# Retrieval gathers in a hybrid decoder step: from 128 tokens by one pick to 64 tokens by two picks

## The reference, cut to what matters

```
pre    = einsum('thkd,td->thk', u_tab[expert], t)      # a dot product per token and pick
act    = gelu(pre) * softmax(top_s)                    # the gate of the pick
y[t]   = einsum('thk,thkd->td', act, v_tab[expert])    # weighted sum of 128 V rows
x      = x + y
```

## Time and profile before

| what | value |
|---|---|
| runs, median (lowest, highest) | 3408.7 us (3402.18, 3413.93) |
| profiled execution, span from first to last instruction | 3400.1 us |
| around the span, against the median | 8.6 us |
| PE busy | 2863.5 us (84%) |
| DVE busy | 2339.7 us (69%) |
| ACT busy | 1195.4 us (35%) |
| POOL busy | 1270.1 us (37%) |
| mean granted TensorE clock | 0.935 |
| moved by DMA | 1225.95 MB, mean 361 GB/s |

### The profile page before, as it was taken

How to read it: one execution, slowest core, us unless ns; L and a number is a source line. 1 busy time by engine, 2 the same in 40 slices (tenths; PEclk the granted TensorE clock), 3 DMA queues, 4 the chain that set the end, 5 groups by cost and what they waited for, 6 DMA issues and landing times.

```text
span 3400.1 us, 31764 instructions
## 1 busy us (share of the span) xinstructions
PE 2863.5 (84%) x9786; PEld 1646.9 (48%) x9786; DVE 2339.7 (69%) x5016; ACT 1195.4 (35%) x3524; POOL 1270.1 (37%) x1102
## 2 busy tenths in 40 slices
PE   8888997888988798787988898788789787888887
PEld 7767764555564356354732365355455232322222
DVE  4454799786778788787566787767668776755444
ACT  3211355332323432443233432432333343334333
POOL 0100233554434443444334433344334343434342
PEclk9899998997899999899999999897889899899999
DMA  4205698999999999999999999999999999999997
GB/s 158 73 8 204 246 390 313 370 375 386 393 406 420 378 413 384 374 381 399 413 421 421 387 407 387 360 345 417 365 410 411 386 419 421 383 422 419 421 422 314
DMA packets 186076, 1225.95 MB, mean 361 GB/s; under 512 B 21281, under 2 KB 23857, under 8 KB 50738
## 3 DMA queue, kind: packets, MB, share of 16 engines
q0 software_dynamic: 152976, 1114.74, 80.8%
q1 hardware_dynamic: 32930, 109.19, 8.5%
HBM read 1212.00 MB, written 11.84 MB: 360 GB/s over the span
## 4 chain that ended last, share of the span: by engine, by line
PE 42%; DMA 29%; DVE 17%; ACT 5%; issue 3%; DVEq 3%; POOL 1%; SPq 0%; ACTq 0%; POOLq 0%
PE ps L601 41%; DMA ring<-in_uv,picked 27%; DVE ring L2329 5%; DVE otok L2263 1%; DVEq L2104 1%; ACT diag L1175 1%; POOL ring L584 1%; ACT scratch L1175 1%; ACT L1175 1%; DVE scratch L2062 1%; ACT gated L1175 1%; DVE keep L1599 1%; ACT act_v L1175 1%; DMA wring<-in_weights 1%; DVE scratch L2066 0%
## 5 line engine op out<-in xcount | busy, mean ns | idle before, releaser
L601 PE MATMUL ps<-ring,diag 128*128 128x512 f32 (+1 forms) x3348 | 1715.6, 645 | 362.6 <-ACT diag L1175 350.4
L584 POOL DMA_INDIRECT ring<-in_uv,picked x1024 | 1184.9, 1157 | 1769.1 <-PE ps L601 1254.1
L2329 DVE SCALAR_TENSOR_TENSOR ring<-ring,htok 128x1024 f32<-128x1024 f32 x1024 | 1249.7, 1227 | 626.5 <-DMA ring<-in_uv,picked 619.2
L601 PEld LDWEIGHTS ps<-ring,diag 128*128 128x128 f32 (+1 forms) x3348 | 619.8, 199 | 1212.8 <-ACT diag L1175 665.7
L1175 ACT ACTIVATE act_v<-pre 128x1 f32<-128x1 f32 x1040 | 210.2, 202 | 1685.7 <-DVE ring L2329 1671.8
L601 PE MATMUL ps<-hT,wring 128*128 128x256 f32 (+1 forms) x3200 | 752.4, 390 | 26.5 <-DVE hT L1562 8.8
L601 PEld LDWEIGHTS ps<-hT,wring 128*128 128x128 f32 x3200 | 618.1, 194 | 200.6 <-issue 96.3
L1175 ACT ACTIVATE diag<-masks,gated 128x128 f32<-128x128 f32 x821 | 329.6, 402 | 27.2 <-PE ps L601 0.2
L1175 ACT ACTIVATE gated<-act_v,gates 128x1 f32<-128x1 f32 x1024 | 301.7, 295 | 33.3
L2263 DVE SCALAR_TENSOR_TENSOR otok<-ring,gated,otok 128x1024 f32<-128x1024 f32 x197 | 252.2, 1280 | 1.1 <-ACT gated L1175 1.1
L601 PEld LDWEIGHTS ps<-scratch 128*128 128x128 f32 (+2 forms) x1428 | 190.5, 196 | 99.5 <-issue 59.5
(11 more groups left out here) (337 smaller groups left out, 1521.1 us busy)
## 6 DMA issues: line engine op xcount, KB each, us to landing
wring<-in_weights SPq DMA_DIRECT2D x200, 512.0 KB
ring<-in_uv,picked POOLq DMA_INDIRECT x1024
scratch<-in_keys POOLq DMA_DIRECT2D x4, 1024.0 KB
scratch<-in_s_gla POOLq DMA_DIRECT2D x4, 1024.0 KB, 12.9
out_o_gla<-scratch POOLq DMA_DIRECT2D x4, 1024.0 KB, 11.1
scratch<-in_s_dn POOLq DMA_DIRECT2D x1, 2048.0 KB, 12.4
scratch<-in_s_ssm POOLq DMA_DIRECT2D x1, 2048.0 KB, 16.7
out_o_dn<-scratch POOLq DMA_DIRECT2D x1, 2048.0 KB, 11.1
```

The source lines that it names most:

```text
L584: pool.indirect_dma_start(out=ring[:, g % RING, :], out_offset=None, in_=io["uv"][L], in_offset=bass.IndirectOffsetOnAxis(ap=index, axis=0 ...
L601: return pe.matmul(out, lhsT, rhs, start=start, stop=stop)
L2329: stt(x, x, 1.0, h, MUL, MUL, accum_out=pre[:, g % SMALL:g % SMALL + 1]).then_inc(sem("dotted"), 1)
```

## The change

Every gather now holds 64 tokens twice: partitions 0 to 63 get one pick of the 64 tokens, partitions 64 to 127 another pick of the same 64 tokens. A unit becomes two half tiles (SUBS, 16 in all, bank w%2 for half tile w) of 64 gathers each, and the number of gathers stays 1040. In the table of picks a group of two heads gives 16 gathers. The matrix of gated values is `diag` of 128x64, made from `folded` (two 64x64 identities stacked), so one product sums both picks. The two 512-column products go to the PSUM partitions 0 to 63 (columns 0 to 511 of the V row) and 64 to 127 (columns 512 to 1023) of one bank. SHARE, add_v and join_out are gone.

What goes with it: `htok[:, 1 + w % 2]` holds the 64 rows twice, made by two 64-column products for each half row from `htok[:, 0]` (fold_rows) and two ACT copies; POOL waits for v_done alone; at the third gather of a half tile ACT copies the sums of the one before to `otok` (copy_out), at the fifth PE transposes them (turn, 4 transposes) and DVE adds them to `xT` (add_out); picks and gates are written to `ids` and copied in four pieces each (fold_choice); the sample tokens' V rows are summed by eight products with one moving column each (sample_v) and the sample rows are spread by eight 128-column products; the last half tile alone is normed in token order, 512 columns wide over all partitions; some slots move by 1 to 4 gathers.

```diff
-SHARE = {0: "21111111", 1: "11123100", 2: "01221112", 3: "22100000", 4: "01221111", 5: "11222100"}
...
+HALF = 64
+SUBS = 2 * len(UNITS)
...
+COPY_AT, TURN_AT, FOLD_AT = 2, 4, 6
...
-EVEN_B, ODD_A, ODD_B = 0, 260, 521
+EVEN_B, ODD_A, ODD_B = 0, 261, 525
...
-        diag = sb("diag", [P, DIAGS, P])
+        diag = sb("diag", [P, DIAGS, HALF])
+        folded = sb("folded", [P, HALF])
...
-                    if g >= RING and ASIDE[g - RING]:
-                        pool.wait_ge(sem("side_done"), SUMMED[g - RING + 1])
-                    elif g >= RING:
-                        pool.wait_ge(sem("v_done"), TURNED[g - RING + 1])
+                    if g >= RING:
+                        pool.wait_ge(sem("v_done"), g - RING + 1)
...
-                for t in range(2):
+                for b in range(2):
                     for c in range(KD):
-                        last = pe.transpose(ps[:, 4 + 2 * t + c // 4, (c % 4) * P:(c % 4 + 1) * P],
-                                            hT[:, c, t * P:(t + 1) * P], ident)
-                    last.then_inc(sem("htok_mm"), 1)
+                        for s in range(2):
+                            last = mm(ps[HALF * s:HALF * s + HALF, 4 + 2 * b + c // 4, (c % 4) * P:(c % 4 + 1) * P],
+                                      hT[:, c, HALF * b:HALF * b + HALF], ident)
+                    last.then_inc(sem("fold_mm"), 1)
+                for c in range(KD):
+                    last = pe.transpose(ps[:, c // 4, (c % 4) * P:(c % 4 + 1) * P], hT[:, c, P:2 * P], ident)
+                last.then_inc(sem("htok_mm"), 1)
...
+            def turn(w):
+                pe.wait_ge(sem("otok_ready"), w + 1)
+                for c in range(4):
+                    last = pe.transpose(ps[:, w % 2, c * P:(c + 1) * P],
+                                        otok[:, 512 * (w % 2) + c * P:512 * (w % 2) + (c + 1) * P], ident)
+                last.then_inc(sem("out_mm"), 1)
+
+            def fold_rows(w, rows):
+                for s in range(2):
+                    last = mm(ps[HALF * s:HALF * s + HALF, w % 2, :], ident[:, HALF * (w % 2):HALF * (w % 2) + HALF], rows)
+                last.then_inc(sem("fold_mm"), 1)
...
+            def tile_v(g, w, k):
+                d, at = TILE_G.index(g) % DIAGS, D
                 for h in range(2):
+                    last = mm(ps[HALF * h:HALF * h + HALF, w % 2, :], diag[:, d, :],
+                              ring[:, g % RING, at + 512 * h:at + 512 * h + 512], k % HALF == 0, k % HALF == HALF - 1)
+                last.then_inc(sem("v_done"), 1)
+
+            def sample_v(g, b):
+                for c in range(KD):
+                    last = mm(ps[:, 3, HALF + c * NS_TOK + b:HALF + c * NS_TOK + b + 1],
+                              ring[:, g % RING, D + c * P:D + (c + 1) * P], gated[:, g % SMALL:g % SMALL + 1])
+                last.then_inc(sem("v_done"), 1)
...
-                if u:
-                    pe.wait_ge(sem("added"), u)
...
+            def copy_out(w):
+                act.wait_ge(sem("v_done"), SUB_FIRST[w + 1])
+                if w > 1:
+                    act.wait_ge(sem("out_mm"), w - 1)
+                f(otok[:, 512 * (w % 2):512 * (w % 2) + 512], ps[:, w % 2, :], ACT.Copy).then_inc(sem("otok_ready"), 1)
...
+            def fold_choice(to, what, slot, g0, g1):
+                v = ids[:, what, :].rearrange("p (g s j) -> p g s j", s=2, j=TOPK)
+                for b in range(2):
+                    for r in range(2):
+                        cp(to[HALF * r:HALF * r + HALF, slot, b, g0 * TOPK:g1 * TOPK].rearrange("p (g j) -> p g j", j=TOPK),
+                           v[HALF * b:HALF * b + HALF, g0:g1, r, :])
...
-            def add_v(g):
...
-            def join_out(u):
...
-                    if g >= 2 and ASIDE[g - 2]:
-                        add_v(g - 2)
-                    if j == 0 and u and HAS_ASIDE[u - 1]:
-                        join_out(u - 1)
-                    if j == 1 and u:
-                        add_out(u - 1)
+                    if g == SUB_FIRST[w] + TURN_AT and w:
+                        add_out(w - 1)
```

More of the change, by code:

```diff
@@ L136, in step_off, with rows_off, fold_slot @@
     return 5 + i // TOPK_AT[u][1]
+def rows_off(u):
+    off = part_off(u, 3) + 2 if u in BESIDE else 5
+    return max(off, FIRST[ROW_TILE[u] - 1] + FOLD_AT + 7 - TOPK_AT[u][0])
+def fold_slot(w):
+    at = SUB_FIRST[w - 1] + FOLD_AT
+    if w > 2 and w % 2 == 0:
+        v = [v for v in range(len(CHOICES)) if ROW_TILE[v] == w // 2 and CHOICES[v][1] != S][0]
+        at = max(at, topk_slot(v, rows_off(v)) + 3)
+    return at
 AHEAD = 8
@@ L1131, in _ @@
+            def sample_v(g, b):
+                for c in range(KD):
+                    last = mm(ps[:, 3, HALF + c * NS_TOK + b:HALF + c * NS_TOK + b + 1],
+                              ring[:, g % RING, D + c * P:D + (c + 1) * P], gated[:, g % SMALL:g % SMALL + 1])
+                last.then_inc(sem("v_done"), 1)
+            front, choose, fold = Strand(mixers()), Strand(choice()), Strand(folds())
             front.upto(-1)
             choose.upto(-1)
+            pe.wait_ge(sem("htok_ready"), 1)
@@ L1165, in _ @@
-                last.then_inc(sem("out_mm"), 1)
+                    if t == S:
+                        pe.wait_ge(sem("gated"), g + 1)
+                        sample_v(g, k)
+                    else:
+                        if g == SUB_FIRST[w] and w > 1:
+                            pe.wait_ge(sem("fold_ready"), 2 * w)
+                        pe.wait_ge(sem("weighed"), TILE_G.index(g) + 1)
+                        tile_v(g, w, k)
+                    fold.upto(g + LEAD)
+                    front.upto(g + LEAD)
@@ L1170, in _ @@
             last.then_inc(sem("ssq_ready"), 1)
+            pe.wait_ge(sem("rows_squared"), 1)
+            for s in range(2):
+                last = mm(ps[HALF * s:HALF * s + HALF, 4, 0:1], folded[:, :], row_sum[:, 0:1])
+            last.then_inc(sem("last_rows_mm"), 1)
         @block.scalar
@@ L1461, in choice, with folds @@
                     f(v, v, ACT.Exp).then_inc(sem("best_exp"), 1)
-            front, choose = Strand(mixers()), Strand(choice())
+            def folds():
+                for w in range(2, SUBS):
+                    for h in range(2):
+                        yield fold_slot(w) + 1 + 4 * h
+                        act.wait_ge(sem("fold_mm"), 2 * w - 1 + h)
+                        act.wait_ge(sem("dotted"), SUB_FIRST[w - 1])
+                        f(htok[:, 1 + w % 2, 512 * h:512 * h + 512], ps[:, w % 2, :], ACT.Copy).then_inc(sem("fold_ready"), 1)
+            def copy_out(w):
[3 more added lines that the diff above has]
+                f(otok[:, 512 * (w % 2):512 * (w % 2) + 512], ps[:, w % 2, :], ACT.Copy).then_inc(sem("otok_ready"), 1)
+            front, choose, fold = Strand(mixers()), Strand(choice()), Strand(folds())
             front.upto(-1)
@@ L1485, in _ @@
+                        f(diag[:, d % DIAGS, :], folded[:, :], ACT.Copy, scale=gated[:, s:s + 1]).then_inc(sem("weighed"), 1)
+                    if g == SUB_FIRST[w] + COPY_AT and w:
+                        copy_out(w - 1)
+                    fold.upto(g)
                     front.upto(g)
                     choose.upto(g)
[L1487 to L1490 removed]
@@ L1544, in first_norm @@
                 dve.wait_ge(sem("base_loaded"), 32)
+                for r in (slice(0, HALF), slice(HALF, P)):
+                    cp(folded[r], ident[r, r])
                 yield from scale_rows(0, 0)
```

278 lines of the change are left out of this document (116 added, 162 removed).

## The result

| | before | after |
|---|---|---|
| median, us | 3410.5 (3402.18 to 3413.93, 4 runs) | 3373.72 (3365.73 to 3379.31, 4 runs) |
| after / before | | 0.9888, 95% interval 0.9866 to 0.991 |
| profiled span, us | 3400.1 | 3371.3 |
| span + what lies around it, us | | 3373.29 |
| granted clock, mean | | 0.84 |

The change makes the kernel 37 us faster. The time around the span is 2 us; I had taken 8.6, by setting the span of one execution beside the median of others. So the two profiles differ by 28.8 us of span, and the rest of the 37 us is that the profiled execution of before was its fastest.

A forecast was written before the change was run, and what follows sets the result against it. The prediction took DMA as the bound, with 118 us of its time unused in the middle. A gain of 48 us there less 3.5 at the start gave -44, a span of 3356 and, with 8.6 around it, 3365 us; range 3318 to 3412.

The forecast's parts named there:

- The price of the pair: V product on TensorE: both halves overlap fully, so a pair costs 0.86 us instead of 1.72.
- the busy sum: TensorE's V time: 1412 us become 881, plus 254 us for changes of shape, -277 us.
- VectorE's sum: VectorE's busy time: rows aside and sums go, small copies come, -249 us; counts only in the holes.
- ScalarE: ScalarE's busy time: more weight matrices, fold copies and copies out, +55 us on an engine at 35%.
- The holes: Gaps in the middle's DMA stream: earlier releases and fewer rows aside give 38 us, plus 10 us in crumbs outside them.
- Gathers beside the projections stay level: Some 250 gathers in 140 projection blocks: TensorE at 3.3 us and DMA at 3.2 stay level, no gain counted.
- The start: Before the first V product: 64-column products and transposes and a ScalarE copy add 3.5 us, bounds 0 and 7.
- The end: After the last gathers: one V pair and one addition less, one product more, -0.5 us, taken as 0.
- What lies around the span: Time outside the profiled span: 8.6 us, added to a forecast span of 3356 us.
- The serial case: Rival: the halves run one after another, 1.72 us a pair for all 1024 gathers; 3480 us, chance 0.06.
- The clock case: Rival: TensorE idles more, its clock drops and waits at projection starts lengthen; 3400 to 3450 us, chance 0.07.
- The case of holes that don't close: Rival: holes come from VectorE's choice and waits the change doesn't shorten; gain 10 less 3.5, 3402 us, chance 0.17.

The follow-up runs named there:

- e7: Changed kernel with a pair of zero-matrix products added behind the V pair in 689 gathers, to keep TensorE busier: 3434.12 us, ratio 1.0077.
- e10: Changed kernel with VectorE operations added behind 203 dots and those gathers' V products and weight matrices left out: 3412.74 us, ratio 0.9995 to the kernel before.
- e13: Kernel before, wide V products kept, with 197 of its 203 VectorE sums shrunk from 1024 columns to one: 3386.9 us, ratio 0.9917.
- e5: Changed kernel with both halves of every V product sent to partitions 0 to 63, so they cannot overlap: 3654.18 us, ratio 1.073 to the kernel before.
- e9: The changed kernel run again unaltered, in the third set: 3376.9 us, ratio 0.9895 to the kernel before.
- e3: Kernel before with no V row on VectorE, all 1024 through TensorE as wide products: 3510.16 us, ratio 1.0285.

## Why the prediction was right, and what was wrong in it

The time (3365.0 forecast, 3373.7 measured) and the sign came out, the stretch that holds the gain too. The sum had 44 us off a profiled span that lost 28.8. That the number came so near is in part luck: the largest term is laid to the wrong engine, and the 48 us it gave were twice what the profile shows.

- **The price of the pair: right; the busy sum: not.** The halves overlap (1.08 us for four passes, 280 us dearer without it). At the clock of 0.947 in e7 all V rows take 1134.7 us, and my sum was 881 + 254 = 1135, but that agreement is chance: the profile counts a pair to its modelled end, and 1024 x 1.08 = 1106 us already without any change of shape. In the changed kernel they take 1345.2, since I priced them at the full clock, and not near half of 1685.7: TensorE's busy time in the middle fell by 147 us, from 2524.30 to 2377.75, and not by 277. The changes of shape showed beside the projections, where 1600 products went from 383.6 to 410.3 us.
- **VectorE's sum: right.** -249 forecast; 2142.85 became 1910.69, -232. ScalarE +55 forecast, and 1098.71 became 1136.37, +38.
- **The holes: the term that failed, in its cause and in its size.** I gave 38 + 10 us, nearly all to TensorE's earlier release, and counted VectorE's relief only where a row aside of 1.28 us stood in a hole, in a third of the holes, some 11 us. The middle gained 24.6 us in the profile. e10 and e13 give the shares the other way round: between nothing and 10 us for the narrow product by itself, 28 (20 to 37) for the relief by itself. The row that should have told me is in the earlier trace rows: DVE at 4.61 of 5 us in the hole. I read it as one place; it is 92% over the 150 us around it as well.
- **"Gathers beside the projections stay level":** not refuted. TensorE's load counts there (e7, e5), and the change left TensorE's time about as it was: 531.46 us of the 612 from 388 to 1000 before, 527.71 after.
- **The start: +3.5 us forecast, +2.4 to +2.8 measured.** POOL's first release comes at 387.79 us instead of 388.37:

```profile
388.37 2.02 POOL L584 DMA_INDIRECT ring<-in_uv,picked  x1 [31.09 <-PE ps L601]
387.79 0.97 POOL L599 DMA_INDIRECT ring<-in_uv,picked  x1 [30.73 <-PE ps L616]
```

But the chain before the first row products ended 3 us earlier in this execution (346.02 instead of 348.96), which had nothing to do with the change: in e9, the same program, they start at 349.64 and the release comes at 391.40. From the first row product to the release it is 41.8 us in both profiles of the changed kernel, and 39.4, 39.0 and 39.0 in those of the kernel before, e3 and e13. The products of 64 columns took 3.71 us as priced (64 passes), the transposes 1.09.
- **The end: 0 forecast, -3.6 us measured** (19.6 to 16.0 us after the last dot's start).
- **What lies around the span: 8.6 us taken, 2 measured.** With 2, the forecast for the profiled execution would have been 3358, and it measured 3373.3: the miss is 15 us and not 9.
- **The rivals.** The serial case at 3480 us was far too cheap: e5 measured 3654. I had priced only the 250 gathers of projections, but e5 loses everywhere outside the last stretch (gathers 52 to 208 take 510.2 us instead of 460.7, and 208 to 780 take 1855.5 instead of 1673.0). The clock case happened in part: the mean in the middle fell from 0.94 to 0.83, most where only gathers run, and there it cost nothing. "A mean clock well under 0.935 with longer projections" was one of my signs of being wrong; the clock did fall, and the projections took 410.3 instead of 383.6 us, but no cost shows where the clock fell most. The case of holes that don't close had it right that they come from the choice and from the mixer's waits, and wrong that nothing in the change shortens them: the rows aside that left VectorE did.

Not settled: what the low clock costs in the busy stretches; how the relief of VectorE turns into time; what the shape changes without it between dots 612 and 740; why a product 0.9 us shorter per gather is worth so little while VectorE is full. That VectorE is then late with the dot in any case would fit, but no run here isolates it.

## What to carry to other kernels

When work moves from one engine to another and gets cheaper on the way, price the two separately: here what the narrow product saved was room on TensorE, and most of the time came from what could leave VectorE. Read busy shares over the stretch around a hole and not only in it or over the whole span; an engine at 92% for 150 us is worth relieving there, though the page says 69%. Spreading the steps of such an engine by their cost instead of their count was worth 17.5 us without changing any work, nearly half of what the whole change brought.

## What the runs showed of the hardware that I had not expected

- A lower clock of TensorE can be free: gathers 780 to 1039 take 655.7 to 661.5 us in all these kernels with seven gathers in the ring, while the mean clock in that stretch is anything from 0.69 to 0.98 (with six in the ring, 667.0 us).
- A VectorE operation on one column still takes 0.215 us, a sixth of the 1.28 us for 1024 columns.
- The Trainium skill (TensorEngine Tiling (Array Packing), Key Properties) says that a change of tiling mode drains TensorE. No run here prices the drain by itself. e5 against e3 gives what it comes to together with the added steps and moved slots when V products are long: 144 us with equal V time. The changed kernel has the same steps and is still faster than the kernel before.
